# Gates of a linear recurrence on TensorE: whole-array products with a block-diagonal weight, or 64-row tiles, two heads at a time

## The reference, cut to what matters

```python
def rg_lru(x, w_r, b_r, w_i, b_i, lam):          # x: 512 tokens x 1024 channels = 16 heads x 64
    xh = xf.reshape(bsz, s, LRU_HEADS, LRU_HEAD_DIM)
    r = sigmoid(einsum('bshi,hij->bshj', xh, w_r) + b_r)
    i = sigmoid(einsum('bshi,hij->bshj', xh, w_i) + b_i)
    log_a = -LRU_C * r * softplus(-lam)
    a = exp(log_a)
    mult = sqrt(-expm1(2.0 * log_a))
    u = mult * (i * xf)
    # h[t] = a[t] * h[t-1] + u[t]
```

## Time and profile before

| | |
|---|---|
| median of 3 runs | 886.07 us (886.01 to 886.84) |
| profiled execution | 886.23 us, its span from first to last instruction 884.5 us |
| mean granted TensorE clock | 0.986 |
| TensorE busy | 836.7 us, 4321 products |
| VectorE, ScalarE, GpSimd busy | 342.2, 273.0, 82.1 us |
| DMA | 253.85 MB, mean 287 GB/s |

### The profile page before, as it was taken

One profiled execution on the slowest core, in us unless ns is written; L12 is line 12 of the kernel. 1 busy time (PEld: TensorE's weight loads), 2 busy tenths in 40 slices (PEclk: granted clock), 3 DMA queues, 4 the chain that ended last, 5 costly groups with the idle time before them and its releaser, 6 DMA issues.

```text
span 884.5 us, 10432 instructions
## 1 busy us (share of the span) xinstructions
PE 836.7 (95%) x4321; PEld 527.9 (60%) x4321; DVE 342.2 (39%) x479; ACT 273.0 (31%) x401; POOL 82.1 (9%) x64
## 2 busy tenths in 40 slices
PE   5999999999999999999999999888998898999996
PEld 4888888788888887536535354352352352533685
DVE  6899549962651616511020120101100101015865
ACT  7666346733332226202010100101001001002777
POOL 3436380000000000000000000000000000001000
PEclk9999999999999999999999999999899999999999
DMA  9222222211525764899999999999999999998902
GB/s 260 97 93 96 95 96 96 96 49 49 189 96 207 296 257 179 349 423 425 401 428 426 428 426 429 426 428 428 428 428 428 426 425 430 427 421 347 356 2 95
DMA packets 45334, 253.85 MB, mean 287 GB/s; under 512 B 8868, under 2 KB 9960, under 8 KB 31976
## 3 DMA queue, kind: packets, MB, share of 16 engines
q1 hardware_dynamic: 42696, 248.21, 69.2%
q0 software_dynamic: 2304, 4.20, 1.2%
q10 hardware_dynamic: 288, 0.79, 0.2%
HBM read 246.89 MB, written 10.49 MB: 291 GB/s over the span
## 4 chain that ended last, share of the span: by engine, by line
PE 44%; DMA 14%; issue 1%; DVE 1%; ACT 1%; DVEq 0%; ACTq 0%
PE bank L1459 42%; DMA ring<-in_w_down_e_dram 11%; DMA ring<-in_w_gate_e_dram 3%; PE bank L1689 1%; PE bank L1785 0%; ACT L1046 0%; ACT r_rounded L901 0%; PE bank L1529 0%; DVE pick L1250 0%; DVE r_rounded L439 0%; ACT r L999 0%; ACT L999 0%; ACT junk L887 0%; PE bank L1775 0%; ACT gain L895 0%
## 5 line engine op out<-in xcount | busy, mean ns | idle before, releaser
L1459 PE MATMUL bank<-ring_rounded,ring_rounded 128*128 128x512 f32 (+1 forms) x696 | 245.0, 389 | 0.3 <-DVE ring_rounded L1134 0.3
L1459 PE MATMUL bank<-r_rounded,ring_rounded 128*128 128x512 f32 (+1 forms) x744 | 234.4, 389 | 0.7 <-DVE ring_rounded L1081 0.6
L1459 PEld LDWEIGHTS bank<-r_rounded,ring_rounded 128*128 128x128 f32 x744 | 138.9, 188 | 30.4 <-DVE ring_rounded L1081 0.9
L1459 PEld LDWEIGHTS bank<-ring_rounded,ring_rounded 128*128 128x128 f32 x696 | 130.3, 188 | 28.1 <-issue 1.3
L1459 PE MATMUL bank<-ring,gain 128*64 128x512 f32 x472 | 118.0, 604 | 9.3 <-issue 8.1
L1459 PE MATMUL bank<-ring,hT 128*64 128x512 f32 x400 | 112.3, 624 | 6.7 <-DMA ring<-in_w_down_e_dram 6.7
L1459 PE MATMUL bank<-ring,junk 128*64 128x512 f32 x472 | 115.5, 592 | 0.0
L1459 PEld LDWEIGHTS bank<-ring,gain 128*64 128x64 f32 x472 | 36.1, 138 | 76.3 <-issue 73.5
L1459 PEld LDWEIGHTS bank<-ring,junk 128*64 128x64 f32 x472 | 37.6, 137 | 71.4 <-issue 71.3
L730 POOL DMA_INDIRECT expert_rows<-r,row_i x16 | 16.5, 1032 | 669.3 <-DVE r L1346 669.3
L945 ACT ACTIVATE r<-bank,factor 128x512 f32<-128x512 f32 x16 | 11.0, 687 | 215.2 <-PE bank L1459 215.2
(11 more groups left out here) (226 smaller groups left out, 761.6 us busy)
## 6 DMA issues: line engine op xcount, KB each, us to landing
ring<-in_w_up_e_dram SPq DMA_DIRECT2D x29, 2048.0 KB, 29.6
ring<-in_w_gate_e_dram SPq DMA_DIRECT2D x24, 2048.0 KB, 27.9
ring<-in_w_down_e_dram SPq DMA_DIRECT2D x22, 2048.0 KB, 32.0
ring<-in_w_in_dram SPq DMA_DIRECT2D x18, 1024.0 KB, 7.3
r<-in_w_gate_e_dram SPq DMA_DIRECT2D x5, 2048.0 KB, 27.9
r<-in_w_down_e_dram SPq DMA_DIRECT2D x4, 2048.0 KB, 34.2
ring<-in_w_down_e_dram SPq DMA_DIRECT2D x7, 1024.0 KB, 21.6
ring<-in_w_up_e_dram SPq DMA_DIRECT2D x6, 1024.0 KB, 11.0
```

The lines of the kernel that those rows point to most:

```text
L1459: return nc.tensor.matmul(*a, **k)
```

## The change

The block-diagonal matrices go. `heads` holds the 64 x 64 matrices side by side: rows 0 to 63 of a channel hold the even head, rows 64 to 127 the odd head; columns 0 to 63 and 64 to 127 hold its two gate matrices, `r` first in the even head and `i` first in the odd head (so nothing needs to be zero). TensorE multiplies the upper 64 rows and the lower 64 rows in two separate products, 64 x 128 stationary and 64 x 512 moving elements, the even head into bank 4 (or 6), the odd head into bank 5 (or 7). In the even head's bank the partitions hold `r` then `i`, in the odd head's bank `i` then `r`.

ScalarE therefore applies each sigmoid in two halves of 64 partitions, and those of `i` write the other half of the partitions than they read. The rows of the bias `b_ig` are loaded with their halves swapped, by two DMAs instead of one. The tables `heads`, `heads_high`, `heads_low` are half as wide as `diag` was, the memset and its semaphore are gone.

The rounding of the newest channel (2, 3, 6 and 7) moves on ScalarE from the next pass to between tanh and the square root, and its low part on VectorE from behind the reciprocal to ahead of it.

```diff
+        heads = r3[:, 0:NX * P].rearrange("p (c j) -> p c j", c=NX)
...
-                          b_rg[0].rearrange("(c p) -> c p", p=P), b_ig[0].rearrange("(c p) -> c p", p=P),
+                        swapped = b_ig[0].rearrange("(c two p) -> c two p", two=2, p=HD)
+                        for odd in range(2):
+                            sp.dma_start(vecs[row:row + NX, HD * (1 - odd):HD * (2 - odd)], swapped[:, odd, :]).then_inc(small_in, 16)
...
-                sp.wait_ge(zero_ready, 1)
                 for w, src in enumerate((w_rg, w_ig)):
                     for odd in range(2):
-                        sp.dma_start(diag[64 * odd:64 * odd + 64, :, w, 64 * odd:64 * odd + 64],
+                        at = HD * (w ^ odd)
+                        sp.dma_start(heads[HD * odd:HD * odd + HD, :, at:at + HD],
                                      src[0].rearrange("(c two) i j -> two i c j", two=2)[odd]).then_inc(lru_in, 16)
...
-            nc.gpsimd.memset(diag[:, :, :, :], 0.0).then_inc(zero_ready, 1)
...
-            nc.scalar.activation(diag_high, diag, ACT.Copy).then_inc(diag_high_ready, 1)
+            nc.scalar.activation(heads_high, heads, ACT.Copy).then_inc(heads_high_ready, 1)
...
-            def lru_gates(c):
+            def lru_gates(c, meanwhile):
...
-                after(nc.scalar.activation(lru_t[:, b, :], bank[4 + 2 * b][:, :], ACT.Sigmoid, bias=col(5, c)))
-                nc.scalar.activation(lru_i[:, b, :], bank[5 + 2 * b][:, :], ACT.Sigmoid, bias=col(6, c)).then_inc(i_ready, 1)
+                nc.scalar.activation(lru_t[even, b, :], bank[4 + 2 * b][even, :], ACT.Sigmoid, bias=col(5, c)[even, :])
+                after(nc.scalar.activation(lru_t[odd, b, :], bank[5 + 2 * b][odd, :], ACT.Sigmoid, bias=col(5, c)[odd, :]))
+                nc.scalar.activation(lru_i[even, b, :], bank[4 + 2 * b][odd, :], ACT.Sigmoid, bias=col(6, c)[odd, :])
+                nc.scalar.activation(lru_i[odd, b, :], bank[5 + 2 * b][even, :], ACT.Sigmoid,
+                                     bias=col(6, c)[even, :]).then_inc(i_ready, 1)
                 if c == 0:
                     act.wait_ge(decay_ready, 1)
                 nc.scalar.activation(lru_t[:, b, :], lru_t[:, b, :], ACT.Tanh, scale=decay[:, c:c + 1]).then_inc(tanh_ready, 1)
+                if meanwhile is not None:
+                    xc_split(meanwhile)
                 act.wait_ge(tanh_ready, c + 1)
                 act.wait_ge(sqrt_free, c + 1)
...
-                if t >= 1 and tiles[t - 1][0] == "xa":
+                if t >= 1 and tiles[t - 1][0] == "xa" and (t - 1) % 4 < LAG:
                     xc_split(tiles[t - 1][1])
...
-                    lru_gates(tiles[t - LAG][1])
+                    lru_gates(tiles[t - LAG][1], c if kind == "xa" else None)
...
-            v.tensor_tensor(diag_low, diag, diag_high, ALU.subtract).then_inc(diag_low_ready, 1)
+            v.tensor_tensor(heads_low, heads, heads_high, ALU.subtract).then_inc(heads_low_ready, 1)
...
                 v.tensor_scalar(q, t, -1.0, 1.0, ALU.mult, ALU.add).then_inc(sqrt_free, 1)
+                if meanwhile is not None:
+                    xc_split(meanwhile)
                 dve.wait_ge(sqrt_free, c + 1)
                 after(v.reciprocal(q, q))
-                if meanwhile is not None:
-                    xc_split(meanwhile)
...
-            pe.wait_ge(small_in, 16 * 6)
+            pe.wait_ge(small_in, 16 * 7)
...
-                for w in range(2):
-                    dst = bank[4 + 2 * (c % 2) + w][:, :]
-                    mm(dst, diag_high[:, c, w, :], xc_high(c), start=True, stop=False)
-                    mm(dst, diag_low[:, c, w, :], xc_high(c), start=False, stop=False)
-                    ins = mm(dst, diag_high[:, c, w, :], xc_low(c), start=False, stop=True)
+                for n, (w, x_) in enumerate(((heads_high, xc_high), (heads_low, xc_high), (heads_high, xc_low))):
+                    for odd in range(2):
+                        rows = slice(HD * odd, HD * odd + HD)
+                        ins = mm(bank[4 + 2 * (c % 2) + odd][:, :], w[rows, c, :], x_(c)[rows, :], start=(n == 0), stop=(n == 2))
```

More of the change, by code:

```diff
@@ L53, in build @@
     HALF = D // 2
+    HD = w_rg.shape[2]
     FAR = 4096
@@ L58, in build @@
     TEAMS = NE // TEAM
-    assert NE % 4 == 0 and S == 512 and D == 1024
+    assert NE % 4 == 0 and S == 512 and D == 1024 and 2 * HD == P
     loads = [(which, e) for which in range(2) for e in range(2)]
@@ L124, in h1T @@
             return (r4[:, 0:D], gain[:, :])[i % 2].rearrange("p (k t) -> p k t", k=KD)
-        diag = r3[:, 0:NX * 2 * P].rearrange("p (c w j) -> p c w j", c=NX, w=2)
-        wpool = r3[:, NX * 2 * P:NX * 2 * P + NB * P].rearrange("p (g j) -> p g j", g=NB)
+        heads = r3[:, 0:NX * P].rearrange("p (c j) -> p c j", c=NX)
+        wpool = r3[:, NX * P:NX * P + NB * P].rearrange("p (g j) -> p g j", g=NB)
         scr = ring[:, 5:7, :].rearrange("p s w -> p (s w)")
@@ L136, in build @@
         gel = scr[:, 10 * S:12 * S].rearrange("p (b t) -> p b t", b=2)
-        diag_high = slot_r[7][:, 0:NX * 2 * P].rearrange("p (c w j) -> p c w j", c=NX, w=2)
-        diag_low = r3_r[:, 0:NX * 2 * P].rearrange("p (c w j) -> p c w j", c=NX, w=2)
+        heads_high = slot_r[7][:, 0:NX * P].rearrange("p (c j) -> p c j", c=NX)
+        heads_low = r3_r[:, 0:NX * P].rearrange("p (c j) -> p c j", c=NX)
         def xc_high(c):
@@ L148, in build @@
         xbp = r4[:, :].rearrange("p (g t) -> p g t", g=NB)
-        o = NX * 2 * P + NB * P
+        o = NX * P + NB * P
         wsum = r3[:, o:o + 2 * W].rearrange("p (b t) -> p b t", b=2)
@@ L298, in build @@
         conv_done = sem("conv_done")
-        diag_high_ready = sem("diag_high_ready")
-        diag_low_ready = sem("diag_low_ready")
+        heads_high_ready = sem("heads_high_ready")
+        heads_low_ready = sem("heads_low_ready")
         xc_high_ready = sem("xc_high_ready")
@@ L522, in small_loads @@
                 for v in (conv_w[0].rearrange("w (c p) -> (w c) p", p=P), conv_b[0].rearrange("(c p) -> c p", p=P),
-                          b_rg[0].rearrange("(c p) -> c p", p=P), b_ig[0].rearrange("(c p) -> c p", p=P),
-                          lru_lambda[0].rearrange("(c p) -> c p", p=P), pool_scale[0].rearrange("(c p) -> c p", p=P)):
+                          b_rg[0].rearrange("(c p) -> c p", p=P), None, lru_lambda[0].rearrange("(c p) -> c p", p=P), pool_scale[0].rearrange("(c p) -> c p", p=P)):
+                    if v is None:
+                        swapped = b_ig[0].rearrange("(c two p) -> c two p", two=2, p=HD)
+                        for odd in range(2):
+                            sp.dma_start(vecs[row:row + NX, HD * (1 - odd):HD * (2 - odd)], swapped[:, odd, :]).then_inc(small_in, 16)
+                        row += NX
+                        continue
                     sp.dma_start(vecs[row:row + v.shape[0], :], v).then_inc(small_in, 16)
                     row += v.shape[0]
-                sp.wait_ge(zero_ready, 1)
                 for w, src in enumerate((w_rg, w_ig)):
                     for odd in range(2):
-                        sp.dma_start(diag[64 * odd:64 * odd + 64, :, w, 64 * odd:64 * odd + 64],
+                        at = HD * (w ^ odd)
+                        sp.dma_start(heads[HD * odd:HD * odd + HD, :, at:at + HD],
                                      src[0].rearrange("(c two) i j -> two i c j", two=2)[odd]).then_inc(lru_in, 16)
@@ L804, in lru_gates @@
                     act.wait_ge(scan_done, c - 1)
-                after(nc.scalar.activation(lru_t[:, b, :], bank[4 + 2 * b][:, :], ACT.Sigmoid, bias=col(5, c)))
-                nc.scalar.activation(lru_i[:, b, :], bank[5 + 2 * b][:, :], ACT.Sigmoid, bias=col(6, c)).then_inc(i_ready, 1)
+                even, odd = slice(0, HD), slice(HD, P)
+                nc.scalar.activation(lru_t[even, b, :], bank[4 + 2 * b][even, :], ACT.Sigmoid, bias=col(5, c)[even, :])
[3 more added lines that the diff above has]
+                                     bias=col(6, c)[even, :]).then_inc(i_ready, 1)
                 if c == 0:
@@ L1114, in _ @@
             v.reciprocal(rcount[:, :], rcount[:, :]).then_inc(prm_ready, 1)
-            dve.wait_ge(diag_high_ready, 1)
-            v.tensor_tensor(diag_low, diag, diag_high, ALU.subtract).then_inc(diag_low_ready, 1)
+            dve.wait_ge(heads_high_ready, 1)
+            v.tensor_tensor(heads_low, heads, heads_high, ALU.subtract).then_inc(heads_low_ready, 1)
             def conv(c):
```

3 lines of the change are left out of this document (1 added, 2 removed).

## The result

The changed kernel takes 888.54 us (median of 13 runs, 886.95 to 890.63), the kernel before, run beside it, 886.28 us (13 runs, 885.33 to 888.61). The ratio is 1.0024 with a 95% interval of 1.0013 to 1.0034: slower by some 2 us (2.26 between the medians, 2.1 by the ratio), where 1.0 us faster was forecast, and outside the stated range of 883.8 to 887.9. The profiled execution is the slowest of the 13 (890.63 us, span 888.9), so its trace shows the worst case. The runs fall into three groups: 886.95 to 887.5 (5 runs), 888.1 to 889.36 (5) and 890.46 to 890.63 (3). Their medians are 887.37, 888.76 and 890.53, 1.4 and 1.8 us apart; 3.4 us at half of TensorE's clock cost 1.7. The runs of the kernel before are spread nearly as widely (885.33 to 888.61), so the groups alone don't say what sets them apart.

The account below looks back on a forecast made before the run. TensorE's stream of products (95% busy) was taken as the bound, with ScalarE and VectorE holding each other as second limit; +0.70 − 1.70 = −1.00 us gave 885.1 us, range 883.8 to 887.9.

Parts of the forecast that it names:

- Pairs of 64 rows: TensorE's gates: two row halves run together, three steps of 0.227 us, 0.68 us a channel instead of 1.36.
- Changes of shape: TensorE entering and leaving 64-row products: 0.08 + 0.16 = 0.24 us per channel, leaving a gain of 0.44 us.
- Sigmoids: ScalarE's gates: four half sigmoids of unchanged duration instead of two whole ones, tanh starts 1.16 us later per channel.
- Bias DMA: SyncE's extra load for the bias row: delays later loads by 0 to 0.3 us, taken as 0.15.
- Roundings: Rounding moved behind tanh on ScalarE: 0.02 us stop for the low part, 0.33 us more for channel 3's.
- The moved roundings at +0.35, passed down unchanged: Channels 0 to 3: 0.02 + 0.33 us, part of the 1.66 us delay carried whole to ScalarE's copy.
- What is late next: TensorE stops 2.5 us at tile 10 for ScalarE's copy; then VectorE's second ya product makes tile 13 0.70 us later.
- Channels 4 to 7: TensorE's gates there gain 1.76 us, of which at most 1.70 can be used: −1.70 us.
- The limit: Low part of block 6's second half, ready at 164.13 and wanted at 165.83, caps the usable gain at 1.70 us.
- rival 1: The stop at tile 10 lowers TensorE's clock: 3.4 us at half cost 1.7, giving 886.4 us; chance 0.27.
- Sum: Whole kernel: +0.70 us from channels 0 to 3 and −1.70 from channels 4 to 7 make −1.00 us.
- The rivals: Clock fall 886.4 us (0.27), costlier shape changes 887.2 (0.13), halves in file 887.7 (0.10), cheaper half activations 883.9 (0.10).

Follow-up runs that it names:

- e9: Changed kernel with each channel's six 64-row products issued twice over; 890.99 us (1 run).
- e7: Changed kernel with the three even-head products issued before the three odd-head ones; 889.47 us, ratio 1.0024.
- e4: Changed kernel with the roundings put back where the kernel before has them, 64-row tiles and four sigmoids kept; 887.91 us, ratio 1.0011.
- e6: Changed kernel with two sigmoids of 128 rows per channel instead of four of 64 (values not the reference's); 885.89 us, ratio 0.9995.
- e8: Kernel before with only the roundings moved, whole-array gates kept; 887.19 us, ratio 1.0008.
- e11: Kernel before with the roundings moved and GpSimd's pooling held until channel 3's scan is done; 887.22 us, ratio 1.0003.
- e5: Kernel before with only GpSimd's pooling held until channel 3's scan is done; 885.97 us, ratio 0.9993.
- e3: Changed kernel with GpSimd's pooling held until channel 3's scan is done; 884.91 us, ratio 0.9982.
- e1: Changed kernel with 12 unused filler products on TensorE ahead of its wait before tile 10; 887.43 us, ratio 1.0009.

## Why the prediction was wrong, point by point

- **Pairs of 64 rows**: right, three steps of 0.23 us (e9). The Trainium skill, "TensorE: Matmul & The Clock Gate", part 3, "The mechanism", has row groups run concurrently; the rows agree, and by e7 in either order of issue.
- **Changes of shape**: 0.44 us per group, not 0.24; inside the bounds (0 to 0.78), mis-sized by my use of the router's products. The gain per channel is 0.24 instead of 0.44. The Trainium skill, "TensorEngine Tiling (Array Packing)", "Key Properties", says that a change of mode drains the engine: the price is real, but in all 0.44 us for entering and leaving.
- **Sigmoids**: +1.51 us instead of +1.16 a channel. The duration was right. The step was not: the rows had 0.58 from one sigmoid to a tanh on another buffer, and four halves start 0.70 apart.
- **Bias DMA**: not resolved. Channel 0's first sigmoid starts at 39.43 against 39.37, and the same start varies by 0.2 to 0.3 us among traces of kernels that are alike up to there. **Roundings**, by themselves: 0.36 us of stop at channel 3, as worked out (0.33), and 0.10 instead of 0.02 at channel 2. At channel 1's scan VectorE is 60.91 − 58.94 = 1.97 late instead of 1.66.
- **The moved roundings at +0.35, passed down unchanged**: the step that failed. I let the whole 1.66 us, 0.35 of them the roundings', pass through VectorE's list unchanged from 58.94 to 77.78, and asked what it does to ScalarE and TensorE but not to GpSimd. The sigmoids' part does pass unchanged (e4). The roundings' part does not: it is 1.38 us instead of 0.35 (e6, e8 and the changed kernel alike), since GpSimd's pooling, which ScalarE's copy releases, now begins ahead of VectorE's scan. From there VectorE takes 0.73 more for the scan, 0.85 less for the low parts, 1.12 more for `q`, from start to start 0.98 in sum. Reciprocal of channel 2 and copy are 2.95 late. The hold shows the cause: with it the moves cost 0.39 us (e11 against e5). Before the result this could be seen: `q` of channel 3 took 1.45 us in the trace of before and that of channel 2 0.41, and the earlier trace rows have GpSimd busy for 19.75 of these 42 us. The Trainium skill, "SBUF — State Buffer", "SBUF: two separate sides", states an exclusive lock on a port pair shared by VectorE and GpSimd, for VectorE's instructions with two inputs in SBUF or in a two-port mode: the engine that comes second waits for the other's instruction to end. Which mode `q` runs in no row says; the times agree: `q` starts at 67.53 inside GpSimd's instruction, which ends at 68.77, and ends at 69.06, 0.29 later.
- **What is late next**: right in kind and place. Tile 10, for the copy L817 (now L829), a stop of 2.93 us instead of 2.5; then the second ya product, +2.94 instead of +1.66 (1.66 had made tile 13 +0.70; now it is +1.98).
- **Channels 4 to 7**: −0.98 instead of −1.70, four times 0.24. The limit has the right place, and only e3 meets it, where TensorE is early enough. That it is met there at 164.10 and was worked out as 164.13 is luck: 164.13 was meant against TensorE's own time, and in e3 TensorE is 1.50 us ahead when channel 4 begins, so in its time the limit is 165.60. VectorE doesn't follow it there, because two low parts (L1147) take 3.72 and 2.10 us beside GpSimd's low part of weights (1.60 and 1.53 before).
- **The clock**: this was rival 1, held less likely because my stop was shorter than 2.63 us. The stop was longer, and "shorter" was no protection either: it fell behind 2.20 us in e4. The trace shows two periods behind this stop; in how many of the 13 runs it fell is open. The steps of 1.4 and 1.8 us between the groups would fit one and two periods more than in the fastest, but the kernel before and e1, whose traces have no fall there, are spread nearly as widely.
- **Sum**: predicted +0.70 − 1.70 = −1.00. Measured in the trace +4.70 − 0.98 = +3.72, of which 2.6 to 2.7 is the clock. Without it +1.98 − 0.98 = +1.0. The 2.0 us between −1.0 and +1.0 are 1.03 for the moved roundings (1.38 instead of 0.35), 0.35 for the sigmoids, 0.72 for the gates of channels 4 to 7, and 0.09 less for the bias DMA. So the sizes alone turn a small gain into a small loss, and in the median the loss is about twice that.

The rivals were right to be there, but I added them one by one. A longer chain makes a longer stop, and the clock can fall behind a stop: they hang together, and the range should have held both at once.

## What to carry to other kernels

Where two engines hold each other without a gap and a third works beside them, a delay that moves all three passes down as it is (e4: 1.38 us at the head, 1.38 at the end). A change of order that moves them against each other does not (1.38 us for moves that cost 0.39 with the third engine out of the way). So find what releases the third engine, list what it does beside each instruction, and redo the overlap at the new times. Products saved on TensorE are worth only what the next engine's copy allows, and work is best saved where the chain starts (here the sigmoids, 1.56 us, against 0.24 on TensorE). Before shortening the bounding engine, look for optional work that disturbs its partners: one wait that holds GpSimd's pooling brought the changed kernel from 2.26 us over the kernel before to 1.66 us under it.

## What was not expected of the hardware

- Products in two row halves run side by side even when issued three and three; a group costs 0.44 us beyond its pairs (0.23 each).
- An activation of 64 rows takes as long as one of 128 (0.68 us), and its successor starts 0.70 us after it.
- VectorE beside GpSimd's pooling: one-input `q` 0.41 to 1.53 us, scan 1.22 to 1.95 us. Half a microsecond decides who pays: with the scan 0.10 us ahead it is GpSimd (1.96 us instead of 1.35), with GpSimd 0.49 us ahead it is the scan.
- TensorE's clock does not fall by the length of the stop alone: it fell behind stops of 2.93, 2.89 and 2.20 us, and in the routing, in two of 14 traces, behind 1.04 and 0.62; it stayed up behind 2.41 and 1.52, and in the other twelve traces behind the same stops in the routing.
